# Final sums of a MoE encoder layer: fewer tiles through TensorE, more through GpSimd, and loads in a new order

## What is computed

```python
def encoder(x, ...):
    for l in range(DEPTH):
        ...
        x = x + jnp.matmul(mix, w_out[l])
        xn2 = rmsnorm(x, norm2_g[l])
        x = x + hier_moe(xn2, ...)          # two expert rows per token
    return rmsnorm(x, final_norm_g)

def rmsnorm(x, g):
    x32 = x.astype(jnp.float32)
    y = x32 * lax.rsqrt(jnp.mean(x32 * x32, axis=-1, keepdims=True) + EPS)
    return (y * g.astype(jnp.float32)).astype(x.dtype)
```

## Time and profile before

| | us |
|---|---|
| median of 3 runs | 1166.03 (1163.17 to 1167.06) |
| time of the profiled execution | 1163.27 |
| span of the profiled execution | 1161.5 |
| PE busy in the span | 1139.5 (98%) |
| DVE busy | 862.1 (74%) |
| ACT busy | 688.6 (59%) |
| POOL busy | 258.1 (22%) |
| granted TensorE clock, mean | 0.996 |

### The profile page before, as it was taken

The page is one execution under the profiler, slowest core; times in us unless marked ns, Lnnn a source line. Parts: engine busy times, 40 slices in busy tenths (PEclk is TensorE's granted clock), DMA queues, the critical chain, the costliest instruction groups (busy, mean ns, idle before and its releaser), DMA issues.

```text
span 1161.5 us, 18098 instructions
## 1 busy us (share of the span) xinstructions
PE 1139.5 (98%) x5934; PEld 961.9 (83%) x5934; DVE 862.1 (74%) x1343; ACT 688.6 (59%) x1134; POOL 258.1 (22%) x345
## 2 busy tenths in 40 slices
PE   7999999999999999999999999999999999999997
PEld 7988888888889988887788888888888888888873
DVE  6649510124547866667899999999999999999997
ACT  6342241223337744335687887877878878878754
POOL 2200210001200012223232323323323223233240
PEclk9999989999999999999999999999999999999999
DMA  7312240436969744453999999999999999999989
GB/s 226 88 37 83 91 137 1 128 126 208 308 239 375 248 146 145 146 200 123 402 383 390 392 393 398 385 399 390 388 399 379 391 394 386 396 390 382 396 315 356
DMA packets 110146, 324.09 MB, mean 279 GB/s; under 512 B 22454, under 2 KB 59232, under 8 KB 85520
## 3 DMA queue, kind: packets, MB, share of 16 engines
q1 hardware_dynamic: 93104, 281.79, 65.5%
q0 software_dynamic: 16992, 41.64, 9.3%
HBM read 285.37 MB, written 51.12 MB: 290 GB/s over the span
## 4 chain that ended last, share of the span: by engine, by line
PE 91%; DMA 4%; DVE 3%; ACT 1%; issue 1%; SPq 0%; POOL 0%; ACTq 0%; DVEq 0%; POOLq 0%
PE psum L953 26%; PE psum L955 25%; PE psum L954 25%; PE psum L1237 2%; PE psum L1272 1%; PE psum L1143 1%; PE psum L1078 1%; PE psum L1079 1%; PE psum L1319 1%; PE psum L1311 1%; PE psum L1086 1%; PE psum L1298 1%; DMA units<-mlstm_units 1%; PE psum L1124 1%; PE psum L999 1%
## 5 line engine op out<-in xcount | busy, mean ns | idle before, releaser
L2057 DVE TENSOR_TENSOR e_lo<-e_st,e_hi 128x1024 fp32r<-128x1024 f32 x384 | 447.0, 1224 | 10.6 <-ACT e_hi L1553 10.6
L1553 ACT ACTIVATE e_hi<-e_st 128x1024 fp32r<-128x1024 f32 x384 | 375.8, 1052 | 9.9 <-DMA e_st<-in_expert_w_gate_dram 4.2
L953 PE MATMUL psum<-e_hi,ex_hi 128*128 128x512 f32 x512 | 199.4, 389 | 0.1
L955 PE MATMUL psum<-e_hi,ex_lo 128*128 128x512 f32 x512 | 199.5, 390 | 0.0
L954 PE MATMUL psum<-e_lo,ex_hi 128*128 128x512 f32 x512 | 199.2, 389 | 0.0
L953 PE MATMUL psum<-xT_hi,w_hi 128*128 128x512 f32 (+1 forms) x432 | 151.5, 351 | 2.2 <-DVE w_lo L1693 1.4
L955 PE MATMUL psum<-xT_hi,w_lo 128*128 128x512 f32 (+1 forms) x432 | 149.4, 346 | 0.0
L954 PE MATMUL psum<-xT_lo,w_hi 128*128 128x512 f32 (+1 forms) x432 | 149.4, 346 | 0.0
L953 PEld LDWEIGHTS psum<-e_hi,ex_hi 128*128 128x128 f32 x512 | 96.1, 188 | 20.5 <-issue 0.3
L955 PEld LDWEIGHTS psum<-e_hi,ex_lo 128*128 128x128 f32 x512 | 96.1, 188 | 20.0
L954 PEld LDWEIGHTS psum<-e_lo,ex_hi 128*128 128x128 f32 x512 | 96.1, 188 | 19.9
(11 more groups left out here) (292 smaller groups left out, 1859.8 us busy)
## 6 DMA issues: line engine op xcount, KB each, us to landing
e_st<-in_expert_w_gate_dram SPq DMA_DIRECT2D x64, 1024.0 KB, 8.4
e_st<-in_expert_w_up_dram SPq DMA_DIRECT2D x64, 1024.0 KB, 9.7
e_st<-in_expert_w_down_dram SPq DMA_DIRECT2D x64, 1024.0 KB, 11.0
mlstm_units<-stage SPq DMA_DIRECT2D x18, 640.0 KB, 4.0
w_st<-in_w_in_dram SPq DMA_DIRECT2D x20, 512.0 KB, 4.4
xn_scratch<-xn POOLq DMA_DIRECT2D x20, 512.0 KB, 3.9
e_st<-expert_rows SPq DMA_DIRECT2D x20, 512.0 KB, 7.7
stage<-gate_rows SPq DMA_DIRECT2D x18, 512.0 KB, 6.1
```

Source lines behind the costliest of these rows:

```text
L953: pe.matmul(out, a_hi, b_hi, start=start, stop=False)
L955: return pe.matmul(out, a_lo, b_hi, start=False, stop=stop)
L1553: act.activation(e_hi[:, r, :, :], e_st[:, slot, :, :], ACT.Copy).then_inc(ehi_done, 1)
L2057: dve.tensor_tensor(e_lo[:, r, :, :], e_st[:, slot, :, :], e_hi[:, r, :, :].bitcast(F32), ALU.subtract).then_inc(elo_done, 1)
```

## The change

Three tiles instead of two get their first sum on GpSimd (0, 1, 2). The second sums are split as four on PE (1, 3, 6, 7), three on GpSimd (2, 5, 8; after its two scatters) and three on DVE (0, 4, 9). Each of PE's four has a pair of banks of its own, so no norm has to be waited for; all four first row parts stand ahead of the second ones. The loads of both halves are issued in orders that interleave the engines' tiles, and the slots follow. DVE's second sums for tiles 4 and 9 stand ahead of the norms of tiles 2 and 7.

```diff
+    EARLY_ORDER = (0, 3, 1, 6, 2, 7, 4, 5, 8, 9)
+    EARLY_POOL = (0, 1, 2)
+    EARLY_DVE = (3, 6, 7, 4, 5, 8, 9)
+    LATE_ORDER = (0, 2, 1, 3, 5, 4, 6, 8, 7, 9)
+    ON_PE = (1, 3, 6, 7)
+    LATE_POOL = (2, 5, 8)
+    LATE_DVE = (0, 4, 9)
...
-    ON_POOL = (0, 1)
-    ON_PE = (2, 4, 5, 7, 8, 9)
-    LATE_ORDER = (0, 2, 1, 3, 4, 5, 6, 7, 8, 9)
...
-            for t in range(NT):
+            for n, t in enumerate(EARLY_ORDER):
                 slot = early_slot(t)
-                if t == 0:
+                if n == 0:
                     sp.wait_ge(elo_done, gu_piece(last, 7)[0] + 1)
-                elif t == 4:
+                elif n == 4:
                     sp.wait_ge(elo_done, down_piece(last, 3)[0] + 1)
-                elif t >= 8:
-                    wait_early_sum(sp, t - 8)
+                elif n >= 8:
+                    wait_early_sum(sp, EARLY_ORDER[n - 8])
...
-            def early_sum(t, last):
-                slot = early_slot(t)
-                pool.wait_ge(e_load[slot], early_loads(t, last))
+            def add_rows(t, slot, loads):
+                pool.wait_ge(e_load[slot], loads)
                 pool.sem_inc(pool_past, 1)
                 pool.tensor_tensor(x1[:, t, :], x1[:, t, :], spare(slot), ALU.add).then_inc(f_pool, 1)
...
-            for t in ON_POOL:
-                early_sum(t, 2 * n_half - 1)
+            for t in EARLY_POOL:
+                add_rows(t, early_slot(t), early_loads(t, 2 * n_half - 1))
...
+            for t in LATE_POOL:
+                wait_early_sum(pool, t)
+                add_rows(t, late_slot(t), late_loads(t, 2 * n_half - 1))
...
             keep_warm_late(24)
-            for j in range(3):
-                if j:
+            for j in range(len(ON_PE)):
+                if 0 < j < 3:
                     keep_warm_late(8)
                 first_row_part(j)
             for j in range(len(ON_PE)):
-                if j >= 4:
-                    pe.wait_ge(f_done, ON_PE[j - 4] + 1)
-                if j >= 3:
-                    first_row_part(j)
                 second_row_part(j)
...
-            for t in range(3, NT):
+            for t in EARLY_DVE[1:]:
                 early_sum(t)
-            for t in range(NT + 2):
-                if t < NT and t not in ON_PE:
-                    late_sum(t)
-                if t >= 2:
-                    final_norm(t - 2)
+            late_ahead = {0: 0, 2: 4, 7: 9}
+            for t in range(NT):
+                if t in late_ahead:
+                    late_sum(late_ahead[t])
+                final_norm(t)
```

More of the change, by code:

```diff
@@ L230, in build @@
     gf_b = at("gf_b", ROWS + 4 * KB, [P, D], F32)
-    ON_POOL = (0, 1)
+    EARLY_ORDER = (0, 3, 1, 6, 2, 7, 4, 5, 8, 9)
[5 more added lines that the diff above has]
+    LATE_DVE = (0, 4, 9)
+    LAST_ROUTED, LAST_OUT = 2, 0
     def spare(slot):
@@ L237, in early_slot @@
     def early_slot(t):
-        return t % 8
+        return EARLY_ORDER.index(t) % 8
     def late_slot(t):
         return 2 + LATE_ORDER.index(t)
-    LAST_ROUTED, LAST_OUT = 2, 0
-    ON_PE = (2, 4, 5, 7, 8, 9)
-    LATE_ORDER = (0, 2, 1, 3, 4, 5, 6, 7, 8, 9)
     psum = nc.alloc_psum_tensor("psum", [P, 8, 512], F32)
@@ L482, in early_loads @@
         def early_loads(t, last):
-            return row_loads(early_slot(t), 1 if t < 8 else 2, last)
+            return row_loads(early_slot(t), EARLY_ORDER.index(t) // 8 + 1, last)
         def late_loads(t, last):
@@ L490, in wait_early_sum, with wait_sum @@
         def wait_early_sum(eng, t):
-            if t in ON_POOL:
-                eng.wait_ge(f_pool, ON_POOL.index(t) + 1)
-            else:
-                eng.wait_ge(f_sum, t + 1 - len(ON_POOL))
-        def sums_taken(t):
-            return NT - len(ON_POOL) + sum(x not in ON_PE for x in range(t + 1))
+            if t in EARLY_POOL:
+                eng.wait_ge(f_pool, EARLY_POOL.index(t) + 1)
+            else:
+                eng.wait_ge(f_sum, EARLY_DVE.index(t) + 1)
+        def wait_sum(eng, t):
+            if t in ON_PE:
+                eng.wait_ge(f_pe_sum, ON_PE.index(t) + 1)
+            elif t in LATE_POOL:
+                eng.wait_ge(f_pool, len(EARLY_POOL) + LATE_POOL.index(t) + 1)
+            else:
+                eng.wait_ge(f_sum, len(EARLY_DVE) + LATE_DVE.index(t) + 1)
         def pe_sum(t):
-            return two((2, 4, 0, 6)[ON_PE.index(t) % 4])
+            return two((2, 4, 0, 6)[ON_PE.index(t)])
         def load_half_steps(eng):
@@ L757, in _ @@
                 if slot < 8:
-                    wait_early_sum(sp, slot)
+                    wait_early_sum(sp, EARLY_ORDER[slot])
                 sp.dma_start(spare(slot), y_dram[T + t * P:T + (t + 1) * P, :]).then_inc(e_load[slot], 16)
@@ L1667, in _ @@
             for t in range(NT):
[L1668 to L1673, removed]
+                wait_sum(act, t)
+                total = pe_sum(t) if t in ON_PE else x1[:, t, :].rearrange("p (a n) -> p a n", a=2)
                 if t >= 1:
@@ L2223, in _ @@
             y_half(last_i - 1, 0, down_piece(last_i, 3)[0] + 1)
-            early_sum(2)
+            early_sum(EARLY_DVE[0])
             y_half(last_i, 1, last_piece(last_i, 3)[0] + 1, bank=0)
-            for t in range(3, NT):
+            for t in EARLY_DVE[1:]:
                 early_sum(t)
-            for t in range(NT + 2):
-                if t < NT and t not in ON_PE:
-                    late_sum(t)
-                if t >= 2:
-                    final_norm(t - 2)
+            late_ahead = {0: 0, 2: 4, 7: 9}
[3 more added lines that the diff above has]
+                final_norm(t)
 _INS = ["x_prompt", "x_sample", "norm1_g", "w_in", "pool_w", "pool_scale", "gate_b", "head_norm_g", "w_out",
```

## The result

The changed kernel took 1170.49 us (median of 5 runs, 1169.1 to 1171.13) against 1164.84 (5 runs, 1162.7 to 1167.06): ratio 1.0053, 95% interval 1.0042 to 1.0064. The profiled execution took 1169.1, with a span of 1167.3.

A forecast was written before the change was run, and what follows sets the result against it. PE's order was taken to bound the last stage. Delays of +1.95 before the scatters and +1.72 on PE, with a +0.9 hold later, gave +4.3 at the last norm; +4.2 on the median made 1170.2, range 1166.0 to 1174.0.

The forecast's parts named there:

- Front: Before the scatters: GpSimd's third sum delays DVE's last subtraction, so PE waits; +1.95, bounds 0 and 2.26.
- PE's order: On PE: a fourth first row part ahead of any second part delays the first second part; +1.72.
- From tile 1 to the end: DVE's last stage: nine norms and two sums take 14.94 from taking up tile 1 at 1146.91, ending at 1161.85.
- The held instruction: Last stage: GpSimd's sum of tile 8 holds DVE's sum of tile 4; +0.9, bounds 0 and 2.26.
- the second-sum loads start about 2.15 later: After the first sums: later scatters delay the second-sum loads by about 2.15, putting GpSimd's sum of tile 8 at 1146.85.
- Sum: At the last norm: end at 1162.75 against 1158.45, +4.3; taken as +4.2 for small overlaps.
- A nil front: Rival: GpSimd's third sum does not come between DVE's subtractions before the scatters; +2.2 in all; chance 20%.
- Transfers as the bound: Rival: loads and stores behind the eighth load set the end, not engine order; between -1.2 and 0; chance 6%.
- The collisions' case: Rival: all three GpSimd second sums hit busy DVE, up to two more holds of 2.26; about +7.8, 1173.8; chance 14%.
- One operand in SBUF: Last stage: DVE's norm of tile 1, reading PSUM and one SBUF tile, is untouched by a GpSimd sum; otherwise held 2.1.

The follow-up runs named there:

- e1: Changed kernel with tile 2's first sum back on DVE instead of GpSimd; ratio to the kernel before 1.0014.
- e4: Kernel before with only tile 2's first sum moved to GpSimd, as its third; ratio to the kernel before 1.0002.
- e2: Changed kernel with tile 1's second row part ahead of the fourth first row part on PE; ratio to the kernel before 1.0024.
- e8: Changed kernel with tile 1 as second first-sum load, so tile 9's load is issued before the scatters; ratio to the kernel before 1.0038.
- e5: Kernel before with all ten first sums on DVE, none on GpSimd; ratio to the kernel before 1.0010.
- e6: e5 also without the two groups of eight unread products between PE's first row parts; ratio to the kernel before 1.0005.
- e7: Changed kernel with all first sums and tile 8's second sum on DVE, without PE's two groups of eight unread products; ratio to the kernel before 0.9999.

## Why the prediction was right

The step that decided it is the order on PE and DVE up to tile 1, and both of its terms came out to 0.02. The time itself, 1170.49 against 1170.2, is closer than the reasoning deserves: the median of the kernel before fell by 1.2 with two more runs, and the loss was 5.65 by medians and 5.22 behind the event, 1.0 to 1.5 more than the 4.2 that were forecast. By medians that is just above the forecast's own +3 to +5.5.

- **Front.** Forecast +1.95, measured +1.93; third sum, last `e_lo` of 3.4, second wait of PE as described. e1 takes it back, e4 brings it in alone (+1.60).
- **PE's order.** Forecast +1.72, measured 1.72 (3.65 together with the front); e2 takes it back. That the end gained 1.81 in e2 shows that it hangs on this part. DVE's wait for tile 1 ended at 1147.38, and 1146.91 had been forecast, on a base that was 0.49 earlier: the same to 0.02.
- **From tile 1 to the end.** Nine norms and two sums were to take 14.94. Measured 1147.38 to 1164.17 is 16.79; less the hold of 1.92 it is 14.87.
- **The held instruction** is the term that was mis-sized: "+0.9" for GpSimd's sum of tile 8, measured 1.92. The upper bound of 2.26 was the right case: the load was so late that DVE's sum went first. It failed at "the second-sum loads start about 2.15 later": they began 2.91 later, since I left the scatters' own time unchanged, and tile 8's load landed 3.9 later, since I also left the loads' own times unchanged. The prediction listed what the waits of SP become but did not ask where the load of tile 9 would land now: behind DVE's first sum, beside the scatters. e8, with that load out of the way, ends 1.7 earlier; how much of this is the order and how much the late second load, whose cause is open, no run separates.
- **Sum.** 1.93 + 1.72 + 1.57 = 5.22 at the last norm against 4.3 forecast (1.95 + 1.72 + 0.63). The third number of each is by how much the way from the first second part to the last norm grew; the held norm is 1.0 more than forecast, and the other parts 0.1 less. The last store landed 2.7 after its issue, as forecast.
- **The rivals.** A nil front is excluded by the trace. Transfers as the bound did not act here, where DVE's stores come 1.39 or more apart and the last eight land 2.7 after their issue, but they took back most of e5's gain. The collisions' case came true for one sum in three, as tiles 2 and 5 fell on an idle DVE.
- **One operand in SBUF.** `ht_lo` took 0.69 beside a GpSimd sum in the changed kernel as well. The norm of tile 1 (PSUM and `gf_b`) shows it in e8: it took its usual 1.28 from 1149.60 to 1150.88, wholly inside GpSimd's sum of tile 8 (1148.82 to 1151.19), so it was not held. The Trainium skill, "SBUF — State Buffer", "Who interferes with whom", has two SBUF inputs against a GpSimd read as the pair that excludes; here the three instructions that were held (`e_lo`, a sum, a norm from SBUF) all have two.

## What to carry to other kernels

Before work is moved to GpSimd, look at what DVE runs at that moment: an add of two SBUF tiles there can hold a DVE instruction with two SBUF inputs for up to 2.26 us, while DVE's own add costs 1.13. Here such an add held up nothing while DVE was idle or worked from PSUM, 0.24 in e8, where DVE asked late in GpSimd's turn, and 1.92 in the changed kernel, more than it saved. Where the end hangs on a result of an engine that runs in order, every instruction put ahead of it costs its full length (1.72 here), also when it saves work later. And when a load is made to wait for another engine's result, ask what transfer it will then run beside.

## What the runs showed of the hardware

- GpSimd and DVE, each with two operands in SBUF, took strict turns in the changed kernel: three GpSimd sums and three DVE subtractions alternated (3.39 and 3.36 on GpSimd, 3.42 and 3.39 on DVE, each the length of the other's turn and its own). Durations of such rows include the wait. With one operand in PSUM, DVE was not held (1.28 in e8, 0.69 in the changed kernel).
- A scatter of 512 KB landed in 3.3 to 3.4 us where the last load had landed before it or within 0.9 of its issue (before, e4, e8), and in 3.9 to 5.4 in the nine other kernels, where one or two 512 KB loads were issued within 0.3 us of a scatter.
- After a wait of 3.75 us PE's granted clock fell to 0.51 for 3.5 us (e6); after waits of 1.29 and 1.65 (changed) and 1.26 and 1.44 (e7) it stayed at 1.00.
- The second of the second-sum loads landed 1.2 to 3.9 us after the first, where the next ones mostly follow at about 1.27. What sets this is open; no run was made for it. In the changed kernel, which had the 3.9, it is part of why tile 8's load was late.
